# Layer 0 of a two-layer block: projections from x times the norm's weights, the norm's root applied at the banks, and one weight unit made in four pieces

## The reference, cut to what matters

```python
h = rmsnorm(x, norm_mix_g[0])      # x * rsqrt(mean(x*x)+eps) * g
proj = h @ a_w_in[0]
qk, v, o, gates, q_mem = split(proj)
qk = silu(causal_dwconv(qk, a_conv_w, a_conv_b))      # 4 taps along the rows
gates = gates + a_gate_b
mk, mv = split(mem @ mem_w_kv[0])                      # keys and values of 256 memory rows
mem_out = memory_attention(q_mem, mk, mv)
hm = mlstm(q, k, v, ...); mix_out = hm * sigmoid(o)
x = x + concat(mix_out, mem_out) @ a_w_out
```

## Time and profile before

| | us |
|---|---|
| median of 3 runs | 1412.67 |
| lowest and highest | 1412.58, 1414.0 |
| the profiled execution, its time | 1412.01 |
| its span in the trace | 1410.2 |

### The profile page before, as it was taken

How to read it: one execution, slowest core, us unless ns; L and a number is a source line. 1 busy time by engine, 2 the same in 40 slices (tenths; PEclk the granted TensorE clock), 3 DMA queues, 4 the chain that set the end, 5 groups by cost and what they waited for, 6 DMA issues and landing times.

```text
span 1410.2 us, 25315 instructions
## 1 busy us (share of the span) xinstructions
PE 1376.1 (98%) x9708; PEld 1231.1 (87%) x9708; DVE 1110.4 (79%) x1713; ACT 760.6 (54%) x1038; POOL 31.1 (2%) x34
## 2 busy tenths in 40 slices
PE   8999999999999999999999999999999999999997
PEld 7897989999988889999899888889999889888886
DVE  6897788888876788888876775687888769777776
ACT  6545555555655555555567644565555544554443
POOL 0001100000000000000000000100000000100000
PEclk9999999999999999999999999999999999999999
DMA  8436747667454346766622232267766655655550
GB/s 319 159 126 236 295 150 252 254 244 250 149 206 146 122 177 246 255 248 237 245 91 75 90 146 79 105 255 255 253 238 245 235 206 191 262 190 182 203 182 30
DMA packets 39402, 276.00 MB, mean 196 GB/s; under 512 B 4496, under 2 KB 4624, under 8 KB 6672
## 3 DMA queue, kind: packets, MB, share of 16 engines
q1 hardware_dynamic: 38016, 266.35, 51.9%
q0 software_dynamic: 1008, 7.86, 1.5%
q10 hardware_dynamic: 288, 0.52, 0.1%
HBM read 273.67 MB, written 1.05 MB: 195 GB/s over the span
## 4 chain that ended last, share of the span: by engine, by line
PE 81%; DVE 12%; ACT 4%; issue 2%; DMA 1%; SPq 0%; DVEq 0%; POOL 0%; ACTq 0%
PE L L2125 20%; PE D L2085 17%; PE L L2316 15%; PE L L2322 8%; PE N L2316 5%; DVE wlo L1144 4%; PE D L2705 3%; PE N L2322 3%; ACT whi L579 2%; PE D L2707 1%; PE D L2245 1%; PE D L2276 1%; DVE arena L1241 1%; PE M L2185 1%; PE D L2316 1%
## 5 line engine op out<-in xcount | busy, mean ns | idle before, releaser
L1144 DVE TENSOR_TENSOR wlo<-raw,whi 128x2048 fp32r<-128x2048 f32 x106 | 242.1, 2284 | 53.6 <-ACT whi L579 53.5
L2316 PE MATMUL L<-h_all,whi 128*128 128x512 f32 x960 | 241.0, 393 | 1.7 <-issue 1.7
L1330 DVE TENSOR_TENSOR wlo<-raw,whi 128x2048 fp32r<-128x2048 f32 x96 | 219.5, 2287 | 28.8 <-ACT whi L709 28.8
L579 ACT ACTIVATE whi<-raw 128x2048 fp32r<-128x2048 f32 x106 | 202.1, 1909 | 60.5 <-PE L L2125 44.3
L2125 PE MATMUL L<-h_all,whi 128*128 128x256 f32 (+1 forms) x992 | 204.9, 304 | 5.0 <-DVE wlo L1510 1.7
L2316 PEld LDWEIGHTS L<-h_all,whi 128*128 128x128 f32 x960 | 173.4, 189 | 33.5 <-issue 2.0
L709 ACT ACTIVATE whi<-raw 128x2048 fp32r<-128x2048 f32 x96 | 183.0, 1907 | 18.8 <-PE L L2322 18.6
L2125 PEld LDWEIGHTS L<-h_all,whi 128*128 128x128 f32 x992 | 159.1, 191 | 16.2 <-issue 7.0
L2125 PE MATMUL L<-h_all,wlo 128*128 128x256 f32 (+1 forms) x496 | 146.8, 300 | 0.0
L2322 PEld LDWEIGHTS L<-h_all,wlo 128*128 128x128 f32 x960 | 130.7, 190 | 9.2
L2085 PE MATMUL D<-hd_hi,whi 128*128 128x256 f32 x480 | 136.0, 283 | 0.8 <-DVE arena L1369 0.8
(11 more groups left out here) (385 smaller groups left out, 2505.7 us busy)
## 6 DMA issues: line engine op xcount, KB each, us to landing
raw<-in_units SPq DMA_DIRECT2D x250, 1024.0 KB, 4.8
arena<-in_band POOLq DMA_DIRECT2D x1, 2304.0 KB, 9.0
arena<-in_nax POOLq DMA_DIRECT2D x1, 1536.0 KB, 6.9
raw<-in_units SPq DMA_DIRECT2D x4, 256.0 KB, 5.1
x<-in_x SPq DMA_DIRECT2D x1, 1024.0 KB, 8.3
t<-in_ctx POOLq DMA_DIRECT2D x1, 1024.0 KB, 5.1
arena<-in_ctx POOLq DMA_DIRECT2D x1, 1024.0 KB, 5.0
out<-t SPq DMA_DIRECT2D x4, 256.0 KB, 2.1
```

Of the source, the lines that this page charges most:

```text
L579: A.activation(whi[weight_slot(v)][:], raw[v % RING][:], ACT.Copy).then_inc(unit_hi, 1)
L1144: V.tensor_tensor(wlo[w][:], raw[v % RING][:], whi[w][:].bitcast(FP), ALU.subtract) \
L1330: V.tensor_tensor(wlo[w][:], raw[v % RING][:], whi[w][:].bitcast(FP), ALU.subtract) \
L2316: mm(bank[:], w[0][:, k, part * P:part * P + P], h_all[:, k, 0:512], start=k == 0, stop=False, skip_group_check=True)
```

## The change

Rows are rounded from x times the norm's weights, without the root: ACT's `rows_hi` (an ACTIVATE with a scale per partition) and DVE's `rows_lo`, which other layers have already, take the place of `apply` on both engines, and `t` is no longer written. The root `rs` is applied as the banks are evacuated: in `a_qm`'s evacuation, in `store_av` by a column `rs_col` that two small matmuls of PE (`scale_columns`) turn, in `qk_conv` by a product into a new SBUF tile `y_qk` out of which the taps then read, in `gate_rows`, and in `output_gate`. The gate weights `gw` are multiplied by the norm's weights once, and the gate products read x. The second unit's high and low parts are made in four pieces, PE's `mv0` waits for them pair of blocks by pair, `mk0`'s bank is evacuated first, and the table of Sqrt is loaded by a one-column activation ahead of its need. The order of ACT's unit 3 and the rows is exchanged.

```diff
@@ build: areas, final count @@
         g_col = area(12432, 2, 4)
+        y_qk = area(13472, 2, T)
...
-        N_FINAL = 5
+        N_FINAL = 4
@@ scalar engine (ACT) @@
             for i in range(4):
                 square(x, i)
+            act.wait_ge(raw_full[1], 16)
+            for i in range(4):
+                c = slice(512 * i, 512 * i + 512)
+                A.activation(whi[1][:, c], raw[1][:, c], ACT.Copy).then_inc(R["piece_hi"] if i < 3 else unit_hi, 1)
+            made[0] = 2
+            act.wait_ge(R["ones_set"], 1)
+            A.activation(h_rs[:, 0, 0:1], ones[:, 0:1], ACT.Sqrt)
             upto(2)
             root()
+            act.wait_ge(ld["vec"], 16)
+            for i in range(4):
+                rows_hi(lambda k: vc("mix_g", k), i)
             upto(3)
-            apply()
             jobs("mv0")
@@ vector engine (DVE) @@
-            made[0] = 1
             V.memset(m_rows, 0.0).then_inc(R["rows_clear"], 1)
-            upto(1)
...
+            def values_piece(i):
+                c = slice(512 * i, 512 * i + 512)
+                if i < 3:
+                    dve.wait_ge(R["piece_hi"], i + 4)
+                else:
+                    dve.wait_ge(unit_hi, 2)
+                V.tensor_tensor(wlo[1][:, c], raw[1][:, c], whi[1][:, c].bitcast(FP), ALU.subtract) \
+                    .then_inc(R["piece_lo"] if i < 3 else raw_used[1], 1)
+
+            mk0 = JOBS["mk0"][0]
+            dve.wait_ge(job_done, mk0.number + 1)
+            to_mkv(0, 0)(0, mk0, bank(mk0)).then_inc(job_evac, 1)
+            for i in range(3):
+                values_piece(i)
             stat()
-            jobs("mk0", to_mkv(0, 0))
+            values_piece(3)
+            made[0] = 2
+            upto(2)
             dve.wait_ge(ld["vec"], 16)
-            apply(lambda k: vc("mix_g", k))
+            for i in range(4):
+                rows_lo(lambda k: vc("mix_g", k), i)
+            dve.wait_ge(ld["gate"], 16)
+            V.tensor_tensor(gw[:], gw[:], vc("mix_g", 0, KB).unsqueeze(2).to_broadcast([P, KB, 8]), ALU.mult) \
+                .then_inc(R["gate_w"], 1)
+            upto(3)
             jobs("mv0", to_mkv(0, 1))
+            dve.wait_ge(R["rs_done"], stats[0])
...
                 at = VECS["a_conv"][0] + 10 * n
-                return conv(m_y[n % 2], pair(b[:]),
+                if n:
+                    prior = JOBS[f"a_qk{n - 1}"][0] if n < 3 else JOBS["a_qk"][n - 3]
+                    dve.wait_ge(job_evac, prior.banked + 1)
+                step(V.tensor_tensor(y_qk, pair(b[:]), over_rows(rs[:]), ALU.mult))
+                sync()
+                return conv(m_y[n % 2], y_qk,
...
-                step(V.tensor_tensor(g_row[0:4, 0:2, :], M0[0:4, :].rearrange("p (a b) -> p a b", b=T), bias, ALU.add))
+                scale = rs[0:4].unsqueeze(1).to_broadcast([4, 2, T])
+                step(V.tensor_tensor(g_row[0:4, 0:2, :], M0[0:4, :].rearrange("p (a b) -> p a b", b=T), scale, ALU.mult))
+                sync()
+                step(V.tensor_tensor(g_row[0:4, 0:2, :], g_row[0:4, 0:2, :], bias, ALU.add))
...
-            jobs("a_qm", lambda n, j, b: V.tensor_scalar(qm, pair(b[:]), 0.125, None, ALU.mult))
+            jobs("a_qm", lambda n, j, b: V.scalar_tensor_tensor(qm, pair(b[:]), 0.125, over_rows(rs[:]), ALU.mult, ALU.mult))
             step(V.memset(v_one, 1.0))
+            dve.wait_ge(R["rs_turn"], 1)
+            step(V.tensor_copy(rs_col[:], Dn[2][:, 0:2]))
+            sync()
             def store_av(n):
                 def run(b):
+                    dst = av[:, :, 256 * n:256 * n + 256]
+                    for tb in range(2):
+                        ins = V.tensor_scalar(dst[:, tb, :], b[:, tb * T:tb * T + T], rs_col[:, tb:tb + 1], None, ALU.mult)
+                        if n % 2 == 0 or tb == 0:
+                            step(ins)
                     if n % 2 == 0:
                         half = P if n == 0 else 0
-                        step(V.tensor_copy(v_halves(n), pair(b[:])[:, :, half:half + P].rearrange("p s (c m) -> p s c m", m=64)))
-                    return V.tensor_copy(av[:, :, 256 * n:256 * n + 256], pair(b[:]))
+                        sync()
+                        ins = V.tensor_copy(v_halves(n), dst[:, :, half:half + P].rearrange("p s (c m) -> p s c m", m=64))
+                    return ins
...
             def output_gate(n):
-                V.tensor_copy(ao[:, 2 * n:2 * n + 2, :], pair(bank(j)[:])).then_inc(job_evac, 1)
+                V.tensor_tensor(ao[:, 2 * n:2 * n + 2, :], pair(bank(j)[:]), over_rows(rs[:]), ALU.mult).then_inc(job_evac, 1)
@@ tensor engine (PE) @@
-            jobs("mv0")
+            def values_ready(k):
+                if k < 6:
+                    pe.wait_ge(R["piece_lo"], k // 2 + 4)
+                else:
+                    pe.wait_ge(*used(1))
+
+            job(JOBS["mv0"][0], True, ready=values_ready)
...
             def gate_products():
-                pe.wait_ge(ld["gate"], 16)
+                pe.wait_ge(R["gate_w"], 1)
                 pe.wait_ge(R["rows_clear"], 1)
                 for i in range(2):
                     for g in range(4):
-                        ins = mm(m_rows[32 * g:32 * g + 8, :], gw[:, 2 * g + i, :], t[:, 2 * g + i, :],
+                        ins = mm(m_rows[32 * g:32 * g + 8, :], gw[:, 2 * g + i, :], x[:, 2 * g + i, :],
                                  start=i == 0, stop=i == 1)
...
+            def scale_columns():
+                pe.wait_ge(R["rs_done"], stats[0])
+                for tb in range(2):
+                    ins = mm(Dn[2][:, tb:tb + 1], rs[0:1, tb * P:tb * P + P], ones[0:1, 0:1], start=True, stop=True)
+                ins.then_inc(R["rs_turn"], 1)
...
-            attention(T_A, 0, 0, 0, NARROW, BESIDE_A, {4: gate_fold}, lead=True)
+            attention(T_A, 0, 0, 0, NARROW, BESIDE_A, {4: gate_fold}, lead=True, begin=scale_columns)
```

More of the change, by code:

```diff
@@ L436, in build @@
         R = {n: sem(n) for n in (
-            "ones_set", "sc_clear", "pick_clear", "ml_fold", "cc_ready", "rows_clear", "ada_out", "ada_turned", "ctx_hi", "ctx_lo", "piece_hi", "piece_lo", "sq_done", "sq_pair", "sq_six", "ss_done", "rv_done", "rs_done", "t_done",
+            "ones_set", "sc_clear", "pick_clear", "ml_fold", "cc_ready", "rows_clear", "ada_out", "ada_turned", "ctx_hi", "ctx_lo", "gate_w", "piece_hi", "piece_lo", "sq_done", "sq_pair", "sq_six", "ss_done", "rv_done", "rs_done", "t_done",
             "h_hi_done", "h_lo_done", "rs_turn", "ctx_t", "gain_sq", "cx_sq", "cx_fold", "cx_ss", "cx_rv", "cx_rs", "sq_fold", "x_ss", "v1_done", "rs1_done", "x_ready", "mod_ready", "q_silu", "o_sig",
@@ L1734, in _ @@
             jobs("b_qm", lambda n, j, b: V.scalar_tensor_tensor(bqm, pair(b[:]), 0.125, over_rows(rs[:]), ALU.mult, ALU.mult), rest_behind=(0,))
-            dve.wait_ge(R["rs_turn"], 1)
+            dve.wait_ge(R["rs_turn"], 2)
             step(V.tensor_copy(rs_col[:], Dn[2][:, 0:2]))
@@ L2230, in residual, with attention @@
                     last_sums()
-            def attention(tl, t0, g0, mixbase, banks, beside={}, after={}, mixed=None, lead=False):
+            def attention(tl, t0, g0, mixbase, banks, beside={}, after={}, mixed=None, lead=False, begin=None):
                 pairs = len(tl) // 2
@@ L2236, in attention @@
                     job(beside[0][1], parts=(0,))
+                if begin:
+                    begin()
                 for s in range(pairs + 2):
@@ L2566, in _ @@
             jobs("b_qm", fresh=True)
-            pe.wait_ge(R["rs_done"], stats[0])
-            for tb in range(2):
-                ins = mm(Dn[2][:, tb:tb + 1], rs[0:1, tb * P:tb * P + P], ones[0:1, 0:1], start=True, stop=True)
-            ins.then_inc(R["rs_turn"], 1)
+            scale_columns()
             def b_mixed(k):
```

## The result

The changed kernel takes 1415.16 us (median of 20 runs, 1413.86 to 1416.14), the kernel before in the same comparison 1412.44 us (20 runs, 1411.74 to 1414.15). The ratio is 1.0017, its 95% interval 1.0011 to 1.0023. So the change makes the kernel slower, by 2.7 us in the medians and by 0.17% in the ratio. That lies inside the 0.2% within which I forecast "no change", and in the forecast range, but it is about twice the +1.3 us of my sum, and the interval of the ratio excludes 1.

A forecast was written before the change was run, and what follows sets the result against it. PE bounds most of the kernel, DVE's chain the stretch from 36 us to the last convolution. A 2.75 us lead against stores, gates' product and six convolutions, less 0.55 absorbed, gave +1.3: 1413.3 profiled, 1414.0 forecast, range 1411.4 to 1416.5.

The forecast's parts named there:

- no change: Whole kernel: 1414.0 us against a median 0.66 us above the profiled execution; within 0.2% (2.8 us), chance 0.78.
- +1.3 us of my sum: DVE's net delay at the last `a_qk` convolution, moving everything behind it as a block: profiled execution 1413.3 us.
- The frame: First 110 us: DVE's chain from first maxima to last convolution takes additions almost in full; lead gone, the rest moves as a block.
- The prices: Costs read from the profile, such as 0.51 us more per convolution, 0.73 for the gates' product, 0.8 for the stores in all.
- The lead: At the start: DVE's first maxima at about 33.45 instead of 36.20, 2.75 us earlier, bounded by 2.2 and 3.2.
- The absorbed 0.55 us: Near 95.43: DVE's old wait for PE's transposed gates absorbs 0.55 us, turning +1.33 into +0.78.
- several waits for the banks of `a_qk`: Sign in the new profile: PE shows several waits for `a_qk` banks that it had only once.
- the product is repaid: Rival at `qk_conv`: each of eight taps loses the price of its bank read, repaying the product; 1411.5 us, chance 0.08.
- the lead survives: Rival up to the scores: DVE's additions lie in waits and PE keeps its 2.9 us; 1409.8 us, chance 0.07.
- The rows come late: Rival at the start: ACT's first row or DVE's third unit slips 1.5 us; +4.0, 1416.7 us, chance 0.13.
- Behind the reciprocal: Rival at the start: PE waits for the piece behind the reciprocal, up to 2 us of lead; about 1415.5, chance 0.04.

The follow-up runs named there:

- E1: Changed kernel with the six convolutions reading their banks directly, without the product with the root (q and k left unscaled): 1411.88 us, ratio 0.9995.
- E2: Changed kernel plus seven matmuls of ones on PE ahead of the third `a_qk` job: 1414.75 us, ratio 1.0014.
- E3: Changed kernel with each `a_qk` bank given back after the product, the Silus waiting for the taps by their own semaphore: 1416.4 us, ratio 1.0029.
- E8: E3 plus 16 matmuls of ones on PE before the first scores: 1413.82 us, ratio 1.0008.
- E4: Changed kernel with fifteen instead of eleven matmuls of ones at the very start: 1417.16 us, ratio 1.0031.
- E11: Changed kernel with the second weight unit whole again, the root still deferred: 1418.82 us, ratio 1.0037.
- E10: E9 with 10 matmuls of ones and ACT's taps of the last two convolutions ahead of its table load, Exp and unit: 1412.6 us, ratio 0.9997.
- E9: E5 plus 9 matmuls of ones on PE before the first scores: 1415.58 us, ratio 1.002.
- E5: E3 with the first tap of four convolutions on ACT, beside DVE's low part of a unit: 1416.46 us, ratio 1.0027.
- E6: Kernel before plus the second unit's four pieces, early copy of `mk0`'s bank and early table load, root not deferred: 1411.53 us, ratio 0.9992.

## Why the prediction was right, and where it was off

**The frame held.** I said that the first 110 us decide, that DVE's chain from its first maxima to the last convolution is what the work is added to, that the lead is used up before the scores, and that the rest moves as a block. The profile after shows each: +3.11 us at the scores, at the feed-forward layer, and 3.2 in the span. E1 shows that the convolutions' root is the item that turns a small gain into the loss.

**The prices held.** Forecast and found: four pieces 2.19 us on ACT from 14.5; convolution 4.22 us and 4.11 (62.93 to 67.04), where the same count gives 3.62 in E1, so 0.49 us more instead of 0.51; six SCALAR_TENSOR_TENSOR 2.72 and 2.71; the pair of TENSOR_SCALAR 0.77 and 0.77 to the next start; product 0.73 and 0.72; the gates' product 0.73 and 0.71; eight rounded rows 3.3 (at 0.41 each) and 3.29. Only the scaled stores were cheaper, 0.19, 0.18 and 0.19 us for n = 0 to 2, together 0.56 where I had 0.8. The rule of the Trainium skill, VectorE: DVE Perf Modes, section Rules for kernel authors, to copy first when many operations follow, did not pay here: one product of 0.72 us bought 0.26 us in one pair of operations, and nothing in the six others.

**The lead was over-sized**: 2.75 us forecast, 1.52 in this profile. I had `mv0` at 16.5; it came at 17.52, since `mk0` ended late at half clock. Where the start kept its full clock (E1, E2, E3, E8) the maxima stand at 33.8 to 34.1, a lead of 2.1 to 2.4, at or just under the low end of my bounds of 2.2 to 3.2; the 1.52 of this profile lies outside them. The rest of the miss is that DVE's column copy waits for `scale_columns`, 0.7 us in E2 and 1.15 in this profile, where I allowed 0.2, and then 0.54 us for the scores, a term that my sum did not have.

**The absorbed 0.55 us is the step whose mechanism failed.** "There 0.55 us are absorbed" took PE to be where it was. But the transposed gates stand behind the jobs that DVE's late bank holds up, and those jobs ran at half the clock. The wait grew to 1.00 us. In E2, with the clock kept, it was gone altogether, as forecast. My sum left the clock out: nothing in it asked what PE does behind a wait that grows to 2.84 us. I had also expected several waits for the banks of `a_qk`; there was this one long one.

Redone with what was measured, the sum closes: -1.52 (lead) + 0.56 (stores) + 0.71 (gates) + 6 x 0.49 + 0.45 (the wait that grew from 0.55 to 1.00) = +3.14 us, against 3.11 found. With E2's start and clock it is -2.11 + 0.56 + 0.71 + 2.94 - 0.55 = +1.55, against 1.60 found (scores at 103.58). Of the 1.8 us between my +1.3 and the +3.11 found, 1.23 are the lead and 1.00 the wait that grew instead of vanishing; stores, gates' product and convolutions came out 0.4 cheaper. So the largest miss is the lead, and half of that is the start's half clock, which the change does not explain. "No change that can be told" came true inside the bound of 0.2%, with 2.7 us of the 2.8 that it allows: that much is luck.

**Of the rivals**, "the product is repaid" and "the lead survives" are out by E1. "The rows come late" is out too: the first rows of ACT start at 20.47 and DVE takes the third unit at 20.58, near the 20.55 and 20.2 that I summed. "Behind the reciprocal" is out: `mv0` runs without a wait.

**What the clock makes in a typical execution.** The profile puts it at 0.9 us behind the third job and 0.6 at the start. The mean clock of every run tells a little more. The kernel before and E2 have 0.999 in their profiled executions, where nothing before 1400 us stands at half clock. None of the 20 runs of the changed kernel reaches 0.999; its four at 0.998 have spans of 1412.6 to 1413.3 us, its ten at 0.995 and 0.996 1413.1 to 1414.3. E2's four runs at 0.999 have 1412.3 to 1412.6, and the eight of the kernel before beside them 1410.2 to 1411.1. My estimate from these is about 1 us for the clock and about 2 us for the work.

**What stays open**: which part of the clock's microsecond is the change's and which the start's, and what brings the late stretches at half clock (145 and 821 us in E4, 149 and 825 in E11, 142 in E1, 818 and 1227 in E10).

## What to carry to other kernels

Before counting a gained lead, look for the engine that will pay for the deferred work, and price the work there: a root moved from eight shared rows to every consumer was done six times on the engine that had no slack. Where two waits end at nearly the same place, measure each half of a change alone: here the root alone was a loss of 6 us (in part the clock's) and the pieces alone probably a gain of 1. One profiled execution can mislead about that, since a transfer that lands late or a stretch at half clock moves it by as much. When a change leaves PE with a longer wait, check the granted clock behind it, and try a few matmuls of ones in the wait: E8 got 2.6 us back for 16 of them, while E9's nine left 2.51 us idle behind them and the clock still fell.

## What the runs showed of the hardware

The granted clock fell to 0.50 around PE's waits, but not by the wait's length alone. It fell with 1.84 (after, at 6.95), 2.38 (E11), 2.51 (E9), 2.84 (after, E4, E11), 4.39 (E3) and 4.52 us (E5). It stayed at 1.00 with 1.72 (before), 1.74 (E3's start), 1.79 (E1), and also with 2.38 in the kernel before and 2.55 in E6. An outright rule on the length of a wait can't be read from these.

Nor does it always fall in the work behind the wait. In the changed kernel it did, 0.4 us after PE had started again at 6.95 and 1.3 us after 84.58. In E3 it fell as PE started again. In E4 it was already at 0.50 while PE still stood idle, ahead of 84.65, and so it was in E11 ahead of 19.47 and of 87.86. E4, by windows:

```profile
84.20:84.60 0.40, 0.00 (x0) 0.00 (x0) 0.40 (x2) 0.06 (x1) 0.00 (x0) 0.50 1.01 430
```

The Trainium skill, TensorE: Matmul & The Clock Gate, section HAM oscillation — how this bites in real kernels, describes the same pattern for waits on transfers: each wait is followed by matmuls at the lower clock. The runs here agree in kind, for waits on another engine, but not for each wait. The cost was about 0.9 us with a wait of 2.84 us (by the profiles of after and E2) and 2.6 us with one of 4.39 (E3 against E8).
